# A delta-net inverse whose turned factor comes from VectorE, and 64x64 products spread over both halves of the partitions

## What is computed

```python
a_mat = jnp.where(strict, einsum('nbhid,nbhjd->nbhij', kb, k) * decay, 0.0)
sol = triangular_solve(a_mat + eye(blk), rhs, lower=True, unit_diagonal=True)
u, w = sol[..., :C_DV], sol[..., C_DV:]
def step(s, xs):
    v_new = u_i - einsum('bhik,bhkv->bhiv', w_i, s)
    o_i = einsum('bhik,bhkv->bhiv', qd_i, s) + einsum('bhij,bhjv->bhiv', qk_i, v_new)
    s = s * gl_i[..., None, None] + einsum('bhik,bhiv->bhkv', kd_i, v_new)
    return s, o_i
```

## Time and profile before

| | |
|---|---|
| median of 3 runs | 1463.69 us |
| the profiled execution | 1466.13 us |
| its span, first to last instruction | 1464.3 us |
| busy over the span | PE 94%, PEld 80%, DVE 53%, ACT 43%, POOL 25% |
| granted TensorE clock, mean | 0.974 |

### The profile page before, as it was taken

The page is one execution under the profiler, slowest core; times in us unless marked ns, Lnnn a source line. Parts: engine busy times, 40 slices in busy tenths (PEclk is TensorE's granted clock), DMA queues, the critical chain, the costliest instruction groups (busy, mean ns, idle before and its releaser), DMA issues. The chain is left out here.

```text
span 1464.3 us, 32200 instructions
## 1 busy us (share of the span) xinstructions
PE 1380.3 (94%) x13336; PEld 1176.4 (80%) x13336; DVE 774.7 (53%) x1400; ACT 629.7 (43%) x1401; POOL 371.9 (25%) x310
## 2 busy tenths in 40 slices
PE   6999999879999999998999978998998999799996
PEld 5999999779999999998999965665765766677785
DVE  5655656512334334336432328876888886444452
ACT  4455545521113212113211117864665666555551
POOL 0022212330322304223132114540011000155553
PEclk9999999989999999999999989999999999899998
DMA  8635445364545245443354434324000013566561
GB/s 238 198 110 168 125 128 164 100 180 140 148 123 127 85 120 152 123 116 101 106 145 129 124 79 142 120 80 124 25 16 1 16 43 94 166 187 201 177 176 61
DMA packets 203639, 177.92 MB, mean 122 GB/s; under 512 B 30440, under 2 KB 189291, under 8 KB 203499
## 3 DMA queue, kind: packets, MB, share of 16 engines
q1 hardware_dynamic: 154489, 118.42, 27.6%
q0 software_dynamic: 28256, 46.35, 11.4%
q10 hardware_dynamic: 20754, 11.14, 2.8%
HBM read 107.79 MB, written 65.59 MB: 118 GB/s over the span
## 5 line engine op out<-in xcount | busy, mean ns | idle before, releaser
L817 PE MATMUL acc<-side_rows,side_w 128*128 128x384 f32 (+2 forms) x2448 | 431.8, 330 | 7.9 <-ACT raw L429 5.3
L817 PEld LDWEIGHTS acc<-side_rows,side_w 128*128 128x128 f32 x2448 | 394.8, 191 | 16.0 <-ACT raw L429 5.4
L2203 DVE TENSOR_TENSOR_SCAN prod<-keepb,prod 128x512 f32<-128x512 f32 (+4 forms) x184 | 203.4, 1147 | 53.9 <-ACT keepb L2129 47.8
L836 ACT ACTIVATE side_stage<-acc 128x384 f32<-128x384 f32 (+2 forms) x102 | 47.1, 462 | 311.4 <-PE acc L817 308.6
L709 PE MATMUL acc<-side_rows,side_w 128*128 128x384 f32 (+1 forms) x864 | 149.3, 330 | 0.0
L709 PEld LDWEIGHTS acc<-side_rows,side_w 128*128 128x128 f32 x864 | 142.4, 188 | 1.9
L1396 DVE COPY base<-b_two 128x512 f32<-128x512 f32 (+1 forms) x45 | 29.8, 662 | 166.1 <-PE b_two L1092 166.1
L2328 PE MATMUL b_y<-whi,mhi 128*128 128x512 f32 x272 | 108.2, 398 | 8.9 <-DVE wlo L2412 7.6
L2147 ACT ACTIVATE wt<-b_w 128x512 f32<-128x512 f32 (+5 forms) x188 | 88.1, 522 | 58.8 <-PE b_w L2061 58.6
L2328 PE MATMUL b_y<-wlo,mhi 128*128 128x512 f32 x272 | 106.7, 392 | 0.0
L2328 PE MATMUL b_y<-whi,mlo 128*128 128x512 f32 x272 | 106.6, 392 | 0.0
(11 more groups left out here) (250 smaller groups left out, 2217.1 us busy)
## 6 DMA issues: line engine op xcount, KB each, us to landing
side_rows<-hs_scratch POOLq DMA_DIRECT2D x16, 1536.0 KB, 11.9
hs_scratch<-side_rows SPq DMA_DIRECT2D x34, 512.0 KB, 4.7
side_rows<-hs_scratch POOLq DMA_DIRECT2D x6, 1344.0 KB, 11.3
base<-in_x_prompt SPq DMA_DIRECT2D x15, 512.0 KB
mixed<-mix_scratch SPq DMA_DIRECT2D x15, 512.0 KB, 6.7
gates<-sz_scratch SPq DMA_DIRECT2D x15, 512.0 KB, 8.0
xres<-in_x_prompt SPq DMA_DIRECT2D x15, 512.0 KB
out_y_prompt<-yy POOLq DMA_DIRECT2D x15, 512.0 KB, 6.6
```

What stands on the lines that cost most here:

```text
L817: last = pe.matmul(self.acc[:, n % 2, 0:width], w[:, w_part, k, :], rows[:, row_part, k, 0:width], start=(k == 0 and i == 0), stop=(k == K ...
L2203: dve.tensor_tensor_scan(prod[0:R, hh, c0:c0 + nk][:, ::-1], kv, kv, prod[0:R, hh, c0 + nk:c0 + nk + 1], ALU.mult, ALU.bypass).then_inc(pr ...
```

## The change

`turn_x` is gone from PE, with its PSUM target and the wait for it in `decay`. DVE turns x itself (`turned`): four transposes per level, each from one half of xc to one half of xh, in blocks of 32x32; xh has the layout of yh now. The copy of y moves from DVE to ACT, to the place where ACT copied the turned x. The state reads and the corrected values choose the half of their output by chunk, head and product; `residual`, `values` (two instructions for one) and `state_part` (three for two) read the halves so chosen.

```diff
+                def state_half(c, h, a):
+                    return (c + h + 1 + a) % 2
+                def value_half(c, h):
+                    return (c + h) % 2
...
-                        def turn_x(g, l):
+                        def level_y(g, l):
...
-                            for a in range(heads_of(g) // 2):
-                                last = pe.transpose(b_xh[:, a, :], xc[:, 2 * a:2 * a + 2, :].rearrange("p h i -> p (h i)"), ident)
-                            last.then_inc(x_turned, 1)
...
-                            pe.wait_ge(xh_kept, NL * g + l)
+                            pe.wait_ge(x_turned, 4 * (NL * g + l))
...
-                                    last = pe.matmul(b_s[at0:at0 + CH, h % 2, o:o + HD], qk_ring[half, m % RING, 2 * a + h // 2, tok],
+                                    last = pe.matmul(b_s[part(state_half(c, h, a)), h % 2, o:o + HD], qk_ring[half, m % RING, 2 * a + h // 2, tok],
...
-                                last = pe.matmul(b_vn[half, 0, h], xt[half, m % 4, h], rr[half, h], start=True, stop=True)
+                                last = pe.matmul(b_vn[part(value_half(c, h)), 0, h], xt[half, m % 4, h], rr[half, h], start=True, stop=True)
...
-                        def keep_turned(g, l):
+                        def keep_y(g, l):
...
-                            act.wait_ge(x_turned, NL * g + l)
-                            act.activation(xh[:, 0:n].rearrange("p a c i -> p (a c i)"), b_xh[:, 0:n].rearrange("p a i -> p (a i)"), ACT.Copy).then_inc(xh_kept, 1)
+                            act.wait_ge(y_ready, NL * g + l)
+                            act.activation(yh[:, :, 0:n, :], b_y[:, :, 0:n, :], ACT.Copy).then_inc(y_kept, 1)
...
-                        def keep_y(g, l):
-                            n = heads_of(g) // 2
-                            dve.wait_ge(y_ready, NL * g + l)
-                            dve.tensor_copy(yh[:, :, 0:n, :], b_y[:, :, 0:n, :]).then_inc(y_kept, 1)
+                        def turned(g, l):
+
+                            h = heads_of(g)
+                            if l == 1:
+                                dve.wait_ge(xt0_ready, 2 * g + 2)
+                            else:
+                                dve.wait_ge(x_new, NL * g + l - 1)
+                            for c in range(2):
+                                for b in range(2):
+                                    dve.transpose(xh[part(b), c, 0:h // 2, :], xc[part(c), b:h:2, :]).then_inc(x_turned, 1)
...
-                            dve.tensor_tensor(vn[half], b_vn[half, 0], cx["beta"][half, m, :].unsqueeze(2).to_broadcast([CH, 4, HD]),
-                                              ALU.mult).then_inc(vn_kept, 1)
+                            for h in range(2):
+                                dve.tensor_tensor(vn[half, h::2], b_vn[part(value_half(c, h)), 0, h::2],
+                                                  cx["beta"][half, m, h::2].unsqueeze(2).to_broadcast([CH, 2, HD]), ALU.mult).then_inc(vn_kept, 1)
```

More of the change, by code:

```diff
@@ L905, in delta_net @@
                 oo = carve(2, 4, CH)
-                xh, yh = carve(4, 2, CH), carve(2, 4, CH)
+                xh, yh = carve(2, 4, CH), carve(2, 4, CH)
                 o_stage = carve(2, P)
@@ L1100, in level_x @@
                                     for b in range(2):
-                                        turned, y = xh[part(b), a, c], yh[part(b), c, a]
+                                        turned, y = xh[part(b), c, a], yh[part(b), c, a]
                                         k_, m_ = (turned, y) if l < NL else (y, turned)
@@ L1106, in read_state @@
                         def read_state(c):
-                            m, at0 = c // 2, (c % 2) * CH
+                            m = c // 2
                             if c:
@@ L1129, in new_values @@
                             if c:
-                                pe.wait_ge(vn_kept, c)
+                                pe.wait_ge(vn_kept, 2 * c)
                             if m and c == 2 * m:
@@ L1140, in update_state @@
                             half = slice(at0, at0 + CH)
-                            pe.wait_ge(vn_kept, c + 1)
+                            pe.wait_ge(vn_kept, 2 * c + 2)
                             for h in range(4):
@@ L1148, in outputs @@
                         def outputs(m):
-                            pe.wait_ge(vn_kept, 2 * m + 2)
+                            pe.wait_ge(vn_kept, 4 * m + 4)
                             for h in range(4):
@@ L1191, in _ @@
                             if new:
-                                turn_x(g, 1)
                                 level_y(g, 1)
@@ L1333, in _ @@
                                 previous_rows(g)
-                                keep_turned(g, 1)
+                                keep_y(g, 1)
                             else:
@@ L1340, in _ @@
                             if new:
-                                keep_turned(g, 2)
+                                keep_y(g, 2)
                             else:
@@ L1348, in _ @@
                                 if new:
-                                    keep_turned(g, l)
+                                    keep_y(g, l)
                                 else:
@@ L1426, in residual @@
                                 o = 2 * HD + (h // 2) * HD
-                                dve.scalar_tensor_tensor(out=rr[half, h], in0=b_s[half, h % 2, o:o + HD], scalar=cx["neg_eg"][half, m, h:h + 1],
+                                dve.scalar_tensor_tensor(out=rr[half, h], in0=b_s[part(state_half(c, h, 1)), h % 2, o:o + HD], scalar=cx["neg_eg"][half, m, h:h + 1],
                                                          in1=vr[half, m % 4, h], op0=ALU.mult, op1=ALU.add).then_inc(r_ready, 1)
@@ L1450, in state_part @@
                             for b in range(2):
-                                dve.tensor_tensor(oo[:, m % 2, b::2, :], b_s[:, b, 0:2 * HD].rearrange("p (a v) -> p a v", a=2),
-                                                  cx["eg"][:, m, b::2].unsqueeze(2).to_broadcast([P, 2, HD]), ALU.mult).then_inc(o_part, 1)
+                                for to, at_ in ((slice(0, P), slice(0, P)),) if b else ((part(0), part(1)), (part(1), part(0))):
+                                    dve.tensor_tensor(oo[to, m % 2, b::2, :], b_s[at_, b, 0:2 * HD].rearrange("p (a v) -> p a v", a=2),
+                                                      cx["eg"][to, m, b::2].unsqueeze(2).to_broadcast([to.stop - to.start, 2, HD]),
+                                                      ALU.mult).then_inc(o_part, 1)
                         def finish(m):
                             dve.wait_ge(o_ready, m + 1)
-                            dve.wait_ge(o_part, 2 * m + 2)
+                            dve.wait_ge(o_part, 3 * m + 3)
                             o = oo[:, m % 2]
@@ L1490, in _ @@
                             if new:
-                                keep_y(g, 1)
+                                turned(g, 1)
                             if old:
@@ L1499, in _ @@
                                 values(c + 1)
+                            if new:
+                                turned(g, 2)
                             split_beside(g, (4,))
-                            if new:
-                                keep_y(g, 2)
                             if old:
@@ L1510, in _ @@
                                 residual(c + 2)
+                            if new:
+                                turned(g, 3)
                             split_beside(g, (6,))
-                            if new:
-                                keep_y(g, 3)
                             if second:
@@ L1520, in _ @@
                                 new_state(c + 2)
+                            if new:
+                                turned(g, 4)
                             split_beside(g, (8,))
-                            if new:
-                                keep_y(g, 4)
                             if second:
@@ L1531, in _ @@
                                 values(c + 3)
+                            if new:
+                                turned(g, 5)
                             split_beside(g, (10,))
-                            if new:
-                                keep_y(g, 5)
                             if second:
```

13 lines of the change are left out of this document (3 added, 10 removed).

## The result

The changed kernel took 1430.24 us, the median of 4 runs (1427.29 to 1431.20), beside 1465.39 for the kernel before (4 runs, 1463.43 to 1468.17). The ratio is 0.9755 with a 95% interval of [0.973, 0.978]: some 35 us faster, where 33.3 were forecast. The profiled execution took 1429.37 us with a span of 1427.5.

What follows compares the result with a forecast made beforehand. PE's queue was taken to bound the delta-net stage; 17.6 + 1.1 (turn) + 7.5 (state reads) + 7.1 (corrected values) = 33.3 us off the 1463.7 median, forecast 1430.5 us, range 1425 to 1437 (72%).

Steps and rivals of the forecast that it cites:

- The turn: PE's turning matmuls ahead of the level product: removal saves 0.44 us in 40 groups, 0.22 in 5 short ones.
- State reads: PE's 34 state reads, spread over four array corners, go from 0.61 to 0.39 us each, saving 7.5 us.
- Corrected values: PE's 34 new-value products, alternating between two corners, go from 0.55 to 0.34 us each, saving 7.1 us.
- DVE: In the delta-net stage DVE goes from 203 to some 273 us busy, about 52%, hidden from PE, cost 0.
- The cover: DVE's free time for turning x before L1103 in the narrowest stretch: 3.57 us remain for 1.78 of transposes.
- ACT: ACT swaps the copy of turned x for that of y: busy time unchanged, about 1 us left before L1103, cost 0.
- The stall: PE's 4.26 us wait before 690.20, behind late weight splits: grows about 0.4, offset by the turn behind it, counted 0.
- The sum: Whole kernel: turn, state reads and corrected values together save 33.3 us, giving a forecast of 1430.5 us.
- Halves that give nothing: Rival: alternating corners on PE do not run side by side, only the turn counts, 18.7 us, 1445; chance 11%.
- A part given back in order: Rival: x or y comes late from DVE and ACT's strict queues, 13 us back, 1443; chance 10%.
- Every split like the one at 682: Rival: all 11 weight splits on DVE come late behind transposes, PE stands 4.3 us each, 47 lost, 1477; chance 4%.
- A turn that PE goes on waiting for: Rival: the level product still waits for turned x, PE's queue stays as long, 1464; chance 3%.

Runs made afterwards that it cites:

- The kernel whose residuals overlap again: The changed kernel with a state read's half chosen by chunk and product alone, all heads alike, and the state part in two instructions: 1430.67 us, ratio 0.9762.

## Why the prediction was right, step by step

- **The turn, 18.7 us: right.** 0.44 per group is what the level product moved by, and the turn alone gave 18.5 in runs; putting it back cost some 18. The choice of 0.44 rather than 0.52 rested on which mode the turn shares, and the two places for the same 170 matmuls bear that reason out; the runs' times alone, 3 us between 0.44 and 0.52, could not.
- **State reads, 7.5 us: right in kind, too small.** The term took 0.39 from L1103 of the half pair, but a read now takes 0.34: 0.27 less per read, 34 x 0.27 = 9.2. The row was badly chosen in one respect: L1103 stands right behind a projection there, while 32 of the 34 reads stand behind another 64x64 group. A read of the kernel before shows what that makes: 0.66 us right behind a projection (844.04 to 844.70), 0.61 behind a level product.
- **Corrected values, 7.1 us: right**, 0.34 as in the earlier trace rows, 7.7 in runs of that part alone.
- **DVE: right.** 271.8 us for 273 forecast, transposes of 439 ns for 445, the residual at its upper end or slightly over it (1.21 to 1.24 for 1.12). **The cover was 3.27 us, not 3.57:** the working took the turn and the new values from PE's side of it and forgot the state read, which stands in the same stretch. The residual starts behind DVE's own add (678.17 + 0.69), so the faster read brought PE's next product nearer and not the transposes. Nothing hung on it here, but doubled transposes came out just beyond it.
- **ACT: right, with less to spare than the row showed.** 1.02 us of slack in the narrow stretch for about 1 forecast, but 0.27 at 444 behind a weight split, the case that was priced at up to half a us. It made no wait; with the transposes doubled it made one, of 0.3.
- **The stall, 0: nearly.** It grew by 0.85 us, where 0.4 was counted and set against the slow turn that went. PE's part, 0.50, was foreseen: the wait ends with a load's landing, so what PE saves ahead of it comes back as wait. The other 0.35 was not: the residual that no longer overlaps puts DVE's split, and with it the load, later. The kernel whose residuals overlap again takes back 0.2 to 0.3 of it.
- **The sum.** With the read as measured and the stall: 18.7 + 9.2 + 7.1 - 0.85 = 34.2, and the stage got 33.9 us shorter. The turn behind the stall took 1.02 (690.20 to 691.22), 0.6 more than its term, so such a sum is good to some 1 us and no better. That the forecast of 33.3 came so near is in part luck: two errors, 1.7 and 0.85, stood on opposite sides.
- **The rivals.** Halves that give nothing (1445) fell by the two runs that change only halves. A part given back in order (1443) fell by PE's waits; of its mechanism there are the 0.35 us in the stall. Every split like the one at 682 (1477) did not come: there is still one such wait, though from a round's second level on the transposes do stand ahead of the splits behind which the copy of y stood. Four times the transposes gave 1527, but by waits for the transposes themselves, so this says nothing on the splits. A turn that PE goes on waiting for (1464) fell by the level product, which starts 0.07 us before the projection's end.

## What to carry to other kernels

Where one engine's queue is the time, take work from it at the price by which the next instruction moves, not at its busy time, and take that price from a row with the same neighbours, since part of it belongs to the change of mode at the border. Before handing work to an engine with time to spare, measure the free stretch between its input and its use in the narrowest level, at every level and with all that becomes shorter on the other engine taken off; a share of 52% or 77% says little. A wait that ends on a transfer eats what is saved ahead of it, so look at it again after each gain.

## What the runs showed of the hardware that was not expected

- Changing between 128x128 and 64x64 work on PE costs some 0.13 us each time by one pair of runs: 0.70 against 0.44 us for the same turn, and 12.4 us over 40 places.
- Eight records of 64x64 that take turns between two halves of the output partitions take 0.34 us, in one half 0.55; sixteen on four corners also take 0.34. The mean of a record doesn't change.
- Four 64x64 instructions of DVE in a row overlap (0.87 us) when their sources lie in one half of the partitions, and don't (1.21 to 1.24) when these alternate; 64-partition transposes run end to end, four of 439 ns in 1.84.
- The same DVE split takes 1.22 us while POOL is idle and 2.2 beside POOL's masks (second split of the pair in the kernel with the split moved first). No run here changes POOL's work alone.
